# Two down transfers of one expert with an outer dimension of eight, waits narrowed to their own operands, and joined gate products

## The reference

```python
# each of the two layers
o_a, o_b, o_c = (branch(...) * silu(z)) @ w_o      # three branches
y = (g0 * o_a + g1 * o_b + g2 * o_c) @ w_out
# last block: forget gates of tokens and of the context
zf, zb = h @ w_in[...], hc @ w_in[...]
# experts: 32 tokens each, width 2752
hid = silu(xs @ w_gate[e]) * (xs @ w_up[e])
y[e] = (hid @ w_down[e]) * gate
```

## Time and profile before

| | us |
|---|---|
| median of 3 runs | 2266.66 |
| lowest, highest | 2264.33, 2267.41 |
| the profiled execution | 2266.97 |
| its span, first to last instruction | 2264.5 |
| PE busy, DVE busy, ACT busy in it | 1774.9, 506.4, 321.8 |

### The profile page before, as it was taken

The page is one execution under the profiler, slowest core; times in us unless marked ns, Lnnn a source line. Parts: engine busy times, 40 slices in busy tenths (PEclk is TensorE's granted clock), DMA queues, the critical chain, the costliest instruction groups (busy, mean ns, idle before and its releaser), DMA issues.

```text
span 2264.5 us, 23719 instructions
## 1 busy us (share of the span) xinstructions
PE 1774.9 (78%) x10250; PEld 1006.1 (44%) x10250; DVE 506.4 (22%) x1135; ACT 321.8 (14%) x750; POOL 51.8 (2%) x91
## 2 busy tenths in 40 slices
PE   7999999999999999997756566566665656665566
PEld 4877785877786686553212222122222212222222
DVE  3264222164223345641000000000100000000001
ACT  1224401224401023320000000000000000000001
POOL 1000000000004000100000000000000000000000
PEclk9999999999999999998777788787877778877788
DMA  9865443455453524389999999999999999999997
GB/s 332 230 218 185 158 162 109 167 205 185 159 207 129 187 91 151 135 357 380 427 429 428 428 427 429 427 427 429 427 428 428 428 428 426 429 427 427 428 428 313
DMA packets 126766, 714.31 MB, mean 315 GB/s; under 512 B 11577, under 2 KB 16249, under 8 KB 96975
## 3 DMA queue, kind: packets, MB, share of 16 engines
q1 hardware_dynamic: 118240, 698.12, 76.1%
q10 hardware_dynamic: 6151, 8.78, 1.3%
q0 software_dynamic: 2272, 5.90, 1.2%
HBM read 708.97 MB, written 3.80 MB: 315 GB/s over the span
## 4 chain that ended last, share of the span: by engine, by line
PE 52%; DMA 45%; SPq 1%; DVE 1%; issue 0%; ACT 0%; DVEq 0%
DMA arena<-in_w_up_dram 22%; DMA arena<-in_w_down_dram 21%; PE banks L873 15%; PE banks L2745 5%; PE banks L1879 5%; PE banks L939 4%; PE banks L1884 3%; PE banks L947 2%; PE banks L2780 2%; PE banks L2792 1%; PE banks L1006 1%; DMA arena<-in_w_mods_dram 1%; PE banks L1034 1%; PE banks L1016 1%; PE banks L959 1%; PE banks L1999 1%
## 5 line engine op out<-in xcount | busy, mean ns | idle before, releaser
L2745 PE MATMUL banks<-arena 128*32 128x512 f32 (+2 forms) x3072 | 423.0, 689 | 326.3 <-DMA arena<-in_w_up_dram 326.3
L2745 PEld LDWEIGHTS banks<-arena 128*32 128x32 f32 x3072 | 133.1, 132 | 584.2 <-issue 583.6
L873 PE MATMUL banks<-arena 128*128 128x256 f32 x1536 | 343.3, 380 | 0.0
L873 PEld LDWEIGHTS banks<-arena 128*128 128x128 f32 x1536 | 287.7, 190 | 42.0 <-issue 5.0
L2780 PE MATMUL banks<-arena 128*32 128x512 f32 x1264 | 204.9, 802 | 88.7 <-DMA arena<-in_w_down_dram 88.7
L2879 DVE SCALAR_TENSOR_TENSOR arena<-arena,banks 64x512 f32<-64x512 f32 (+1 forms) x48 | 30.5, 636 | 511.2 <-ACT arena L2802 510.3
L2780 PEld LDWEIGHTS banks<-arena 128*32 128x32 f32 x1264 | 44.4, 134 | 224.6 <-DMA arena<-in_w_down_dram 122.6
L2802 ACT ACTIVATE arena<-banks 64x512 f32<-64x512 f32 (+1 forms) x48 | 26.7, 556 | 821.1 <-PE banks L2745 819.7
L1879 PE MATMUL banks<-arena 128*128 128x256 f32 x512 | 113.6, 380 | 0.9 <-DVE arena L1388 0.9
L1879 PEld LDWEIGHTS banks<-arena 128*128 128x128 f32 x512 | 96.0, 190 | 14.4 <-DVE arena L1388 1.1
L2886 DVE COPY arena<-banks 128x512 f32<-128x512 f32 x16 | 11.1, 692 | 343.3 <-PE banks L2793 326.4
(11 more groups left out here) (356 smaller groups left out, 1641.6 us busy)
## 6 DMA issues: line engine op xcount, KB each, us to landing
arena<-in_w_gate_dram SPq DMA_DIRECT2D x60, 2752.0 KB, 35.3
arena<-in_w_up_dram SPq DMA_DIRECT2D x60, 2752.0 KB, 32.7
arena<-in_w_down_dram SPq DMA_DIRECT2D x64, 2048.0 KB, 31.4
arena<-in_w_in_dram SPq DMA_DIRECT2D x68, 1024.0 KB, 8.3
arena<-in_w_mods_dram SPq DMA_DIRECT2D x48, 1024.0 KB, 7.4
arena<-in_w_down_dram SPq DMA_DIRECT2D x31, 1024.0 KB, 27.2
arena<-in_w_out_dram SPq DMA_DIRECT2D x12, 1024.0 KB, 5.1
arena<-in_w_gate_dram SPq DMA_DIRECT2D x8, 1376.0 KB, 9.9
```

The lines of the kernel that those rows point to most:

```text
L873: mm = pe.matmul(b[:, i * S:i * S + S], w, rhs[:, kt, :], start=kt == 0, stop=kt == 7)
L2745: mm = pe.matmul(bank[pc][32 * g:32 * g + 32, 0:w_], xsT[:, kt, CAP * e4:CAP * e4 + CAP], (wg if g < 2 else wu)[:, c:c + w_], start=kt == ...
```

## The change

It has four parts.

1. In each layer, the waits ahead of the first scores are for the three jobs before the last three. The wait of the `wo` jobs is for each branch's own four tiles, and the wait for the misc bank stands at branch 1 alone. The first `wout` job waits for each `wo` job of the last branch just ahead of the two blocks that it wrote.
2. Jobs zf and zb take one column tile each, for tokens and context together, in matmuls of 512 columns, since `hT` and `hcT` lie side by side. ACT writes two halves, DVE scales once.
3. For expert 8, each of the two 256-row down transfers gets the source order `b q` of `(q b)` with b = 8: partition 16 b + q receives the row pair 8 q + b.
4. For expert 8, DVE writes the hidden columns that belong to these rows in the same order into `mask`, and `turn` reads tiles 8 and 9 from there.

```diff
+EIGHTHS = 8
@@ PE, layers @@
                         if i2 == 0:
-                            pe.wait_ge(o_read.sem, o_read.at(l, 12))
+                            pe.wait_ge(o_read.sem, o_read.at(l, 4 * br + 4))
+                        if i2 == 0 and br == 1:
                             pe.wait_ge(misc_read.sem, misc_read.at(l, 5))
...
-                        if n == 0:
-                            for i in range(4):
-                                pe.wait_ge(reader(l, JOB_OF["wo", 8 + i]), taken(l, JOB_OF["wo", 8 + i]))
                         for kt in range(8):
+                            if n == 0 and kt % 2 == 0:
+                                i = JOB_OF["wo", 8 + kt // 2]
+                                pe.wait_ge(reader(l, i), taken(l, i))
...
-                for j in range(FIRST_FILL - BANKS, FIRST_FILL):
+                for j in range(FIRST_FILL - 2 * BANKS, FIRST_FILL - BANKS):
                     pe.wait_ge(reader(l, j), taken(l, j))
@@ last block @@
+        hbT = arena[:, q0 + 6144:q0 + 10240].rearrange("p (c k t) -> p k c t", c=2, k=8)
...
+                elif kind in ("zf", "zb"):
+                    for kt in range(2 * quarters[0], 2 * quarters[-1] + 2):
+                        mm = pe.matmul(view(b, 2, S), slot(loads[kt // 4])[:, kt % 4, n * P:n * P + P], hbT[:, kt, :, :],
+                                       start=kt == 0, stop=kt == 7)
...
-                        nc.scalar.activation(dst, view(b, 2, S), ACT.Tanh, scale=0.5).then_inc(reader(L2, j), 1)
+                        nc.scalar.activation(dst[:, S:2 * S], b[:, 0:S], ACT.Tanh, scale=0.5)
+                        nc.scalar.activation(dst[:, 0:S], b[:, S:2 * S], ACT.Tanh, scale=0.5).then_inc(reader(L2, j), 1)
...
-                        for k in range(2):
-                            h_ = 2 * (n % 2) + k
-                            z1 = EZv[:, d, h_, S * (n // 2):S * (n // 2) + S]
-                            ins = nc.vector.tensor_scalar(z1, z1, lb[:, 12 + h_:13 + h_], lb[:, 8 + h_:9 + h_], ALU.mult, ALU.add)
-                        ins.then_inc(own2.sem, own2.up())
+                        z1 = EZv[:, d, n, :]
+                        nc.vector.tensor_scalar(z1, z1, lb[:, 12 + n:13 + n], lb[:, 8 + n:9 + n],
+                                                ALU.mult, ALU.add).then_inc(own2.sem, own2.up())
@@ experts, SP @@
-                            sp.dma_start(slot[:, 2 * D * hf:2 * D * hf + 2 * D],
-                                         w_[r0:r0 + 2 * P, :].rearrange("(p k) c -> p (k c)", k=2)).then_inc(moe_full[s_], 16)
+                            src = w_[r0:r0 + 2 * P, :].rearrange("(p k) c -> p (k c)", k=2)
+                            if e == EIGHTHS:
+                                src = src.rearrange("(q b) x -> b q x", b=8)
+                            sp.dma_start(slot[:, 2 * D * hf:2 * D * hf + 2 * D], src).then_inc(moe_full[s_], 16)
@@ experts, PE @@
-                    mm = pe.transpose(MB[:, b:b + 64], hid[0:64, c], ident[0:64, 0:64])
+                    cols = mask[0:64, (j - 8) * P:(j - 7) * P] if e == EIGHTHS and j in (8, 9) else hid[0:64, c]
+                    mm = pe.transpose(MB[:, b:b + 64], cols, ident[0:64, 0:64])
@@ experts, DVE @@
+                    if e == EIGHTHS and pc == 2:
+                        by8 = lambda a, k: a.rearrange("p (q b k) -> p q b k", b=8, k=2)[:, :, :, k]
+                        for k in range(2):
+                            nc.vector.scalar_tensor_tensor(mask[0:64, k * P:k * P + P].rearrange("p (b q) -> p q b", b=8),
+                                                           by8(bank[pc][64:P, 0:2 * P], k), 0.5, by8(h_[:, 0:2 * P], k), ALU.mult, ALU.mult)
+                        nc.vector.scalar_tensor_tensor(h_[:, 2 * P:], bank[pc][64:P, 2 * P:w], 0.5, h_[:, 2 * P:],
+                                                       ALU.mult, ALU.mult).then_inc(hid_ready.sem, hid_ready.up())
+                        continue
```

More of the change, by code:

```diff
@@ L1865, in job @@
                         mm = pe.transpose(b[:, i * P:i * P + P], xnv[:, t, (4 * hf + i) * P:(4 * hf + i) * P + P], ident)
-                elif kind in ("tq", "tk", "tkc", "tqh") or (kind in ("zf", "zb")):
-                    ctx_ = kind == "tkc" or (kind in ("zf", "zb") and n < 2)
+                elif kind in ("zf", "zb"):
+                    for kt in range(2 * quarters[0], 2 * quarters[-1] + 2):
+                        mm = pe.matmul(view(b, 2, S), slot(loads[kt // 4])[:, kt % 4, n * P:n * P + P], hbT[:, kt, :, :],
+                                       start=kt == 0, stop=kt == 7)
+                elif kind in ("tq", "tk", "tkc", "tqh"):
                     if kind == "tkc" and n == 0:
@@ L1873, in job @@
                             pe.wait_ge(reader(L2, jj), taken(L2, jj))
-                    rhs = hcTv if ctx_ else hTv
+                    rhs = hcTv if kind == "tkc" else hTv
                     for q_ in quarters:
@@ L2118, in _ @@
                     elif kind in ("zf", "zb"):
-                        dst = EZv[:, int(kind == "zb"), 2 * (n % 2):2 * (n % 2) + 2, S * (n // 2):S * (n // 2) + S]
+                        dst = EZv[:, int(kind == "zb"), n, :]
                         act.wait_ge(job_done.sem, made(L2, j))
-                        nc.scalar.activation(dst, view(b, 2, S), ACT.Tanh, scale=0.5).then_inc(reader(L2, j), 1)
+                        nc.scalar.activation(dst[:, S:2 * S], b[:, 0:S], ACT.Tanh, scale=0.5)
+                        nc.scalar.activation(dst[:, 0:S], b[:, S:2 * S], ACT.Tanh, scale=0.5).then_inc(reader(L2, j), 1)
                     elif kind == "gh":
```

## The result

The changed kernel takes **2279.28 us** in the median of four runs (2278.36 to 2282.69), the kernel before 2267.03 beside it (four runs): ratio 1.0054, 95% interval 1.004 to 1.0068. That is 12 us slower, against 9.6 us faster in the forecast (2257.2), and outside its range of 2255.0 to 2265.5. The profiled execution took 2278.66 us for a span of 2276.6.

A forecast was written before the change was run, and what follows sets the result against it. TensorE's chain was taken to bound the time before the expert stage, DMA bytes and their spread over engines the stage itself. Savings of 1.6, 1.6, 3.5 and 2.9 us sum to -9.6: forecast 2257.2 us, range 2255.0 to 2265.5.

The forecast's parts named there:

- Parts 1 to 3: PE's waits before first scores, output products and first L947 job, two layers: shortened, saving 1.6, 1.6 and 3.5 us.
- Part 4: Jobs zf and zb: 512-column matmuls cost the same per column as 256-column ones; 0.9 us counted as nothing.
- Part 5: DVE's product for expert 8 split in three: 0.5 to 1 us more, hidden under PE's waits, so nothing.
- Part 6: Expert 8's two down transfers: eight engines take 256 KB each; if the early ones, the stream's end moves -2.9 us.
- rival A: End of stream: the eight loaded engines are the late ones, or half are; +4.9 for -2.9, 2264.9 us; chance 0.18.
- D: Expert 8's two transfers: rows read 64 KB apart are slower; at three times the price +10.0, 2276.7 us; chance 0.04.
- B: Expert 8's two transfers still spread over 16 engines, so they give nothing: -6.7, 2260.0 us; chance 0.06.
- C: Before 972 us another wait swallows the early savings: -2.9 alone, 2263.8 us; chance 0.04.

The follow-up runs named there:

- e1_early: Changed kernel without its eight-block order for expert 8's two down transfers, early edits kept: 2259.98 us, ratio 0.9966 to the kernel before.
- g4_four: Kernel before, expert 8's two down transfers loading only partitions 0 to 15 and 32 to 47, in four blocks of four: 2263.53 us, ratio 0.9982.
- e2_far8: Kernel before with only expert 8's two down transfers in eight blocks, rows 64 KB apart: 2284.88 us, ratio 1.0076.
- f6_fours: Kernel before, expert 8's two down transfers loading only partitions 0 to 63, in eight-block pieces with four partitions a block: 2268.02 us, ratio 0.9999.
- e3_near8: Kernel before with expert 8's two down transfers in eight blocks, rows 8 KB apart (other rows read): 2288.45 us, ratio 1.0087.
- e4_far16: Kernel before with expert 8's two down transfers in sixteen blocks, rows of an engine 128 KB apart: 2278.10 us, ratio 1.0043.
- eights: Kernel before, expert 8's two down transfers loading only partitions 0 to 63, in eight blocks of eight partitions: 2274.04 us, ratio 1.0026.
- f5_near16: Kernel before with expert 8's two down transfers in sixteen blocks of eight partitions, rows 8 KB apart (other rows read): 2276.34 us, ratio 1.0039.
- f8_odd: Kernel before, expert 8's two down transfers loading only partitions 64 to 127, in eight-block pieces with four partitions a block: 2277.02 us, ratio 1.0039.
- g3_halves: Kernel before with each of expert 8's two down transfers cut at partition 64, same rows in the same order: 2277.15 us, ratio 1.0044.
- g2_one: Kernel before with only the first of expert 8's two down transfers in eight blocks: 2277.28 us, ratio 1.0054.

## Why the prediction was wrong

**What bounds the kernel: right.** What e1_early saved ahead of the expert stage reached the end: in its profile the first expert load and the last bytes both come 5 us sooner than in that of before. Bytes and their spread counted too (g4_four, -3.5 us; the changed kernel, +12).

**Parts 1 to 3: right.** These are the early waits. The waits for L1170, L1620 and L1639 have no row left. The forecast's -6.7 us stands against -8.2 (-4.8 to -10.7 by the interval of the ratio). In the two profiles the first expert load moved by 4.9 us and not by the 6 to 7 that the prediction asked for. But the first layer of the changed kernel's profile began 2.6 us later (the chain that ended last, before and changed):

```profile
54.49 7.10 PE banks L873 x32
57.13 7.10 PE banks L874 x32
```

From there to the first expert load it is 917.4 us before and 909.8 after, 7.5 less. Such starts vary by themselves: eleven of the experiments' kernels are the kernel before up to that load, and their profiles issue it between 973.3 and 975.2 us.

**Part 4: right as nothing.** Twelve records of 512 columns take as long as 24 of 256 (two rows of the chain that ended last):

```profile
794.97 5.18 PE banks L1885 x24
...
801.77 5.15 PE banks L1871 x12
```

L1885, the 256-column jobs that are left, has 256 records and L1871, the joined ones, 128, as foreseen. PE waits for neither ACT nor DVE at L1871.

**Part 5: right.** The two strided products (x2) and the short one run from 1672.01 to 1672.73 us, 0.7 us where one took 0.56, and PE's transposes wait 0.6 us for the last of them (timeline of DVE at expert 8):

```profile
1672.01 0.59 DVE L2892 SCALAR_TENSOR_TENSOR arena<-banks,arena 64x128 f32<-64x128 f32 x2
1672.46 0.27 DVE L2894 SCALAR_TENSOR_TENSOR arena<-banks,arena 64x128 f32<-64x128 f32 x1
```

**Part 6: this is the step that failed,** twice. Its term in the sum was -2.9 us; measured are +16.8 us for e2_far8 against the kernel before, and +19.3 for the changed kernel against e1_early. Eight engines, 256 KB each: right, by the sixteen closing packets fewer. The first error is the rate. "One engine moves 428/16 = 26.75 GB/s" and 128 KB "in **4.9 us**" took the rate of an engine as its own, the same whichever partitions it writes and whatever its neighbours do. The runs show that it holds only for the deal of a plain transfer of 128 partitions (or one that keeps to its places, f6_fours). In this deal the whole stream fell to 226 GB/s. The changed kernel lost, against e1_early's 423, 427 and 428 in the same three stretches, 24 + 201 + 35 GB/s over 20 us each: 5.2 MB, 12.1 us.

The second error is the choice of the eight. I held the early half likelier, called it a judgement, and it was six early ones and two late. Two are enough: the end is set by the last engine, so rival A's +4.9 us holds ("the eight are the late ones, or half of them are"), which I gave 0.18. The sum of the two, 17.0 us, stands against 16.9 between the spans of e1_early (2259.7) and the changed kernel (2276.6), and 19.3 between their medians. By their ends the split is a little different: the stream ends 15 us later (0.00 first at 2248 and at 2263), and the piece behind it is near 2 us longer, as PE is busy for 6.7 us behind the last bytes and not 4.8. Its granted clock was 0.50 from 2258 to 2260 us, where in e1_early it was 1.00 throughout the last step. f6_fours, without a dip but with two late engines and a clock of 0.50 just before, has 6.8 us; no run takes the two apart. Which part of the dip's 12.1 us was made good later (some 2 us of it) no row settles.

**The rivals.** D gave +10.0 us, 2276.7, by rows at three times the price, and said "a dip of GB/s where expert 8's down rows land": the size and the sign were right, the cause was not. Near rows cost as much (e3_near8), far rows in the right places cost nothing (f6_fours). I had priced a row as if it slowed its own engine; rows in the wrong place slowed the packets of the whole stream. The rule that I cited against the change, the outermost size under 16 of the Trainium skill (DMA: Bandwidth & Descriptors, Rules for kernel authors), gives +4.9 us of the about 17; sixteen blocks obey it and still lose 8 to 10 us. What spoke for the larger price was on another page, the port map, and I had not asked which partitions an engine writes before and after the change. B and C fell: the count of packets, and e1_early.

**How far the cause is shown.** Shown: the dip hangs on the places that the engines write, not on their number, the row step, the order of rows or the bytes; and in the dip every kind of packet takes about twice as long. Argued from the skill's map, with no run against it: that the places are ports, and that two engines on one port halve each other. A theory of crowded ports stood already in the expectations of e2_far8, e3_near8 and e4_far16; the map came after them. In the four layouts tried with it (fours low, eights, fours high, halves) and in f5_near16 it told beforehand whether there would be a dip. It did not tell the size: e4_far16, f8_odd, g3_halves and the stream of g2_one all cost more than it had priced. Open: why the other transfers' packets slow as well, so that 2 MB in sixteen blocks cost 9 us and not the 4.9 us that their own bytes at half rate would; and why eight engines are late at all. The 44 instruction fetches of the earlier trace rows are a suspect; no run took them away.

## What to carry to other kernels

The access pattern of a DMA decides three things: how many engines, which, and what partitions each writes. Where a stream runs at the rate of all engines, ask for the third before cutting or reordering a transfer: two harmless halves of 64 partitions cost 10 us here. A skew of engines at the end is mended only if the engines that get more are all early; the DMA share, read as a count of sixteenths, tells how many are left and whether a plan met them. A dip can last longer than its transfers, so half of the bad bytes doesn't mean half of the loss (g2_one). And an edit that pays (the early waits, -8 us) should be timed apart from one that is a bet.

## What the runs showed that I had not expected

- A busy DMA engine says little of its speed: share 1.03 at 226 GB/s, and 1.01 at 428 forty us later.
- 2 MB in badly placed transfers slow the whole stream for 17 to 30 us, other transfers included: 6.77 MB in 28 us where 12.02 passed before, and 1571 ns for a row of a gate or up load instead of 821.
- The late eight are not the eight that a transfer in eight blocks uses, nor the other eight: of those used, six are early and two late, and those two are not among the four that g4_four's transfers use.
